# VectorE's pieces of linear attention two stick-breaking units further back in its program

## What is computed

```
z = einsum(q_blk, k) * scale;  mask = key_pos < q_pos
log_1m_beta = where(mask, log_sigmoid(-z), 0)
between = reverse_cumsum(log_1m_beta) - log_1m_beta
weights = where(mask, exp(log_sigmoid(z) + between), 0);  out = weights @ v

log_alpha = log_sigmoid(gd @ gate_up + gate_b) / 16
b = cumsum(log_alpha)                  # in each chunk of 64 frames
o_inter = (q * exp(b)) @ S
scores[t,s] = sum_k q[t]*k[s]*exp(b[t]-b[s])   for s <= t
S = S * exp(b_last) + (k * exp(b_last - b))^T @ v
o = head_rmsnorm(o_inter + scores @ v, norm_g) * silu(g)
```

## Time and profile before

| what | us |
|---|---|
| median of 3 runs | 1580.3 (1577.7 to 1583.3) |
| profiled execution, own time | 1584.14 |
| its span | 1582.4 |
| TensorE matmul busy, whole span | 1478.7 (93%) |
| VectorE busy, whole span | 661.9 (42%) |
| ScalarE busy, whole span | 523.8 (33%) |
| GpSimd busy, whole span | 305.2 (19%) |
| mean granted TensorE clock | 0.979 of full |

### The profile page before, as it was taken

How to read it: one execution, slowest core, us unless ns; L and a number is a source line. 1 busy time by engine, 2 the same in 40 slices (tenths; PEclk the granted TensorE clock), 3 DMA queues, 4 the chain that set the end, 5 groups by cost and what they waited for, 6 DMA issues and landing times.

```text
span 1582.4 us, 27309 instructions
## 1 busy us (share of the span) xinstructions
PE 1478.7 (93%) x11281; PEld 1143.1 (72%) x11281; DVE 661.9 (42%) x1058; ACT 523.8 (33%) x936; POOL 305.2 (19%) x412
## 2 busy tenths in 40 slices
PE   5989989989898898989999999999999999999997
PEld 4767767766676554554678788888888888888875
DVE  5244152646563253646275424232332424242336
ACT  4432231424223466777343303122120403021121
POOL 5574624413241251514000100000000000000000
PEclk9999989999999899999999999999999999999999
DMA  5554413423233603004332402112020202111015
GB/s 185 140 146 124 125 42 101 116 57 96 57 87 93 178 2 81 2 1 133 111 132 78 144 16 67 40 40 66 13 93 0 93 13 68 38 61 45 27 40 186
DMA packets 134793, 124.10 MB, mean 78 GB/s; under 512 B 20797, under 2 KB 112122, under 8 KB 134698
## 3 DMA queue, kind: packets, MB, share of 16 engines
q1 hardware_dynamic: 88192, 92.69, 19.0%
q10 hardware_dynamic: 46506, 30.04, 6.8%
HBM read 97.88 MB, written 24.84 MB: 78 GB/s over the span
## 4 chain that ended last, share of the span: by engine, by line
PE 46%; DVE 2%; ACT 1%; DMA 1%; issue 1%; POOLq 0%; SPq 0%; DVEq 0%; ACTq 0%
PE all_ps_b L1990 22%; PE all_ps_b L1967 21%; PE all_ps_b L1572 2%; DMA bk_acc<-in_w_out 1%; POOLq L1592 0%; DVE bk_acc L1855 0%; PE all_ps_b L1960 0%; ACT bk_acc L1758 0%; DVE bk_acc L1865 0%; DVE bk_w1L L1826 0%; DVE all_hL L1871 0%; DVE bk_acc L1851 0%; DVE bk_acc L1922 0%; DVE bk_acc L1925 0%; DVE all_gL L1897 0%
## 5 line engine op out<-in xcount | busy, mean ns | idle before, releaser
L1907 DVE TENSOR_TENSOR bk_acc<-bk_acc,all_ps_b 128x512 f32<-128x512 f32 x128 | 87.9, 687 | 285.3 <-PE all_ps_b L1990 285.3
L1967 PE MATMUL all_ps_b<-all_hH,bk_w1L 128*128 128x512 f32 x512 | 200.1, 391 | 5.1 <-PE all_ps_b L1990 2.2
L1990 PE MATMUL all_ps_b<-bk_w2H,all_gL 128*128 128x512 f32 x512 | 199.8, 390 | 2.5 <-DVE all_gL L1897 2.5
L1990 PE MATMUL all_ps_b<-bk_w2L,all_gH 128*128 128x512 f32 x512 | 199.9, 390 | 0.0
L1990 PE MATMUL all_ps_b<-bk_w2H,all_gH 128*128 128x512 f32 x512 | 199.8, 390 | 0.0
L1967 PE MATMUL all_ps_b<-all_hH,bk_w1H 128*128 128x512 f32 x512 | 199.3, 389 | 0.0
L1967 PE MATMUL all_ps_b<-all_hL,bk_w1H 128*128 128x512 f32 x512 | 199.2, 389 | 0.0
L1200 PE MATMUL fr_ps_F<-fr_hH,fr_wL 128*128 128x512 f32 (+1 forms) x416 | 174.8, 420 | 5.7 <-POOL fr_wL L448 5.5
L448 POOL TENSOR_TENSOR fr_wL<-fr_raw,fr_wH 128x256 fp32r<-128x256 f32 (+1 forms) x208 | 159.6, 798 | 32.6 <-ACT fr_wH L495 29.2
L1200 PE MATMUL fr_ps_F<-fr_hL,fr_wH 128*128 128x512 f32 (+1 forms) x416 | 164.4, 395 | 0.0
L1200 PE MATMUL fr_ps_F<-fr_hH,fr_wH 128*128 128x512 f32 (+1 forms) x416 | 164.3, 395 | 0.0
(11 more groups left out here) (339 smaller groups left out, 2234.9 us busy)
## 6 DMA issues: line engine op xcount, KB each, us to landing
fr_raw<-in_w_in ACTq DMA_DIRECT2D x37, 512.0 KB, 4.2
bk_raw<-in_w_ff SPq DMA_DIRECT2D x32, 512.0 KB, 4.3
all_raw<-in_w_ff SPq DMA_DIRECT2D x32, 512.0 KB, 4.8
projected<-fr_stage ACTq DMA_DIRECT2D x39, 256.0 KB, 4.4
fr_raw<-in_w_in SPq DMA_DIRECT2D x13, 512.0 KB, 4.2
fr_xt<-in_x SPq DMA_DIRECT2D x8, 512.0 KB, 5.3
bk_acc<-in_x SPq DMA_DIRECT2D x8, 512.0 KB, 3.3
x_after_mixers<-bk_acc SPq DMA_DIRECT2D x8, 512.0 KB, 2.7
```

The lines of the kernel that those rows point to most:

```text
L1907: dve.tensor_tensor(acc[:, j, ds], acc[:, j, ds], ybank[g % 4][:], ALU.add).then_inc(collected, 1)
L1967: m = pe.matmul(bank[s][h][:], w[s][:, k, :], a[:, k, hs], start=(k == 0 and q == 0), stop=(k == KB - 1 and q == 2))
L1990: m = pe.matmul(ybank[g % 4][:], a[:, i, ts], w[:, i, ds], start=(i == 0 and q == 0), stop=(i == FB - 1 and q == 2))
```

## The change

In VectorE's program of a unit, the linear attention pieces that are issued behind unit u are now those of slots up to u - 2 instead of u. The order of the pieces among themselves, their number, and the programs of all other engines stay. The largest slot is 28 + 26 = 54, so that the last pieces are now issued behind unit 56 of 72, which is unit 8 of the third pair.

```diff
@@ -2747,7 +2747,7 @@
                         scale(i - 1)
                     if i and u == LOW_AT:
                         mixed_low(i - 1)
-                    gla(i * NU + u)
+                    gla(i * NU + u - 2)
 
             for i in range(PAIRS):
                 if i:
```

## The result

| | before | after |
|---|---|---|
| median, us | 1584.16 (6 runs) | 1595.42 (6 runs) |
| lowest and highest, us | 1577.7, 1586.52 | 1591.55, 1599.8 |
| profiled execution: own time, span, us | 1584.14, 1582.4 | 1593.99, 1592.3 |
| mean granted TensorE clock | 0.979 | 0.979 |

The ratio is 1.0074, with a 95% interval of 1.0053 to 1.0096: slower by 11.7 us, 8.4 to 15.2. The direction is the one that was forecast. The time, 1595.4, lies above the forecast 1589.5 and 0.9 us above the upper end of the range. Two things add up to that: the three later runs of before were all at 1585 or more, which moved the base from 1580.3 to 1584.2, and the change cost 11.7 us where 9.2 were forecast. The second is not clear of noise, since 9.2 lies inside the interval of 8.4 to 15.2.

What follows compares the result with a forecast made beforehand. TensorE has almost no air in the stick-breaking and linear attention stage, so new waits cost time: 2.0 + 0.4 + 1.7 + 0.2 + 1.7 + 3.2 = +9.2 us on 1580.3 gives 1589.5 us, range 1582.5 to 1594.5.

Steps and rivals of the forecast that it cites:

- the other pieces: Rest of linear attention, both halves: TensorE finds operands ready within some tenths; +0.4 us (0 to 2).
- place 2: Second pair: earlier units gain, then a stall before transpose L2479 takes it back; +0.2 us, +1.7 for the clock.
- Place 1: First pair: transpose L2479 waits some 2.9 us for VectorE's k·exp product; +2.0 us, +1.7 for the clock.
- The gain ahead of the transpose: Second pair: with shorter waits on softplus, TensorE comes to transpose L2479 some 3.2 us earlier.
- what was gained is waited away: Second pair: the time gained is lost in one stall of some 3.2 us before transpose L2479.
- Place 3: Third pair, end of linear attention: gating 3.1 us later delays the projection's load and conversion L1560; +3.2 us (2.2 to 5).
- (a): Rival, chance 0.16: same waits, but the clock stays up behind them; +5.3 us, 1585.6.
- (b): Rival, chance 0.11: no price in the second pair, as ScalarE's exponentials run earlier too; +4.1 us, 1584.4.
- (c): Rival, chance 0.08: faster, VectorE waits go and ScalarE's conversion waits without holding TensorE; 1570.1 us.
- (d): Rival, chance 0.10: new waits larger by GpSimd's instruction (0.7), longer low clock at each stall; some +14 us, 1594.3.
- the forecast's 1.7: Clock loss behind a TensorE wait of 3 us before the transpose: +1.7 us each in first and second pair (0 to 3.4).

Runs made afterwards that it cites:

- the middle pieces alone: Only keys, state, takes and soft_g stand two units further back, against the kernel before: 1586.9 us, ratio 1.0019.
- the swap of the products: Full change plus VectorE's keys' product (L2355) put ahead of the queries' product (L2351), against the kernel before: 1594.5 us, ratio 1.0066.
- early pieces alone: Only soft, scan, to_last, diag0, diag1, qin, kout stand two units further back, against the kernel before: 1592.5 us, ratio 1.0044.
- the part kernels: Three kernels, each delaying only one group of VectorE's pieces by two units, against the kernel before: ratios 1.0044, 1.0019 and 1.0003.
- the end alone: Only both0, both1, result0, result1 stand two units further back, against the kernel before: 1586.6 us, ratio 1.0003.
- the kernel with only `SPLIT_AT` 9: Kernel before with ScalarE's conversion of the first loaded block one unit later (SPLIT_AT 8 to 9), against the kernel before: 1584.9 us, ratio 0.9991.
- the conversions later: Full change plus SPLIT_AT from 8 to 9, ScalarE's conversions one iteration later, against the kernel before: 1597.0 us, ratio 1.0077.
- the three slots put back: Full change with diag1, qin and kout one unit back instead of two, against the kernel before: 1594.4 us, ratio 1.0064.
- one unit: All pieces one unit further back instead of two, against the kernel before: 1580.9 us, ratio 0.9977.

## Why the prediction was right in direction and short in size

**What failed, in short.** The larger part of the miss is the base: with 1584.2 in place of 1580.3 the forecast of +9.2 us is 1593.4, and the range moved with it, 1586.4 to 1598.4, holds the 1595.4 measured. In the sum the term that was mis-sized is "the other pieces", +0.4 us, put in without stepping through them: 1.9 us by the landmarks, 3.0 (0.5 to 5.5) by the middle pieces alone. The three places were found and have the forecast's sign. In place 2 one step was wrong, and its net came out right by luck.

**Place 1, forecast +2.0 and +1.7: right.** TensorE waits 3.45 us before L2479 where 2.9 were forecast, and the stretch around it grew by 3.8 us against 3.7. VectorE's timeline there:

```profile
555.19 0.42 DVE L2739 SCALAR_TENSOR_TENSOR sb_SP<-sb_E,all_ps_b 128x256 f32<-128x256 f32 x1 [1.38 <-ACT sb_E L2653]
555.53 0.68 DVE L2346 TENSOR_TENSOR gla_A<-all_ps_b,gla_eye 128x512 f32<-128x512 f32 x1
556.13 0.84 DVE L2351 TENSOR_TENSOR gla_qin<-gla_qin,gla_q 128x512 f32<-128x512 f32 x1
556.89 1.09 DVE L2355 TENSOR_TENSOR gla_kout<-gla_kout,gla_k 128x512 f32<-128x512 f32 x1
```

Softplus 10 starts as logarithm 10 ends, then come the three operations, as stepped; they take 2.79 us instead of 2.48. The difference of 0.3 us goes with GpSimd, whose timeline is:

```profile
555.70 0.73 POOL L2589 TENSOR_TENSOR sb_R<-sb_R,sb_SP 128x256 f32<-128x256 f32 x1 [1.98 <-DVE sb_SP L2739]
556.75 0.70 POOL L2427 TENSOR_TENSOR gla_D<-gla_cum 128x256 f32<-128x256 f32 x1 [0.18 <-issue]
557.41 1.17 POOL L2428 TENSOR_TENSOR gla_D<-gla_cum 128x256 f32<-128x256 f32 x1
```

GpSimd's update is released by softplus 10, and its next instructions lie beside q·exp and k·exp, which took 0.84 and 1.09 us instead of 0.69. The Trainium skill, SBUF — State Buffer, "SBUF: two separate sides", has VectorE with two SBUF inputs and GpSimd reading SBUF lock one port pair and the loser wait for a whole instruction: the trace agrees in direction, but the loss was 0.15 and 0.4 us beside instructions of 0.70 and 1.17.

**Place 2, forecast +0.2 and +1.7: right in size, with one step wrong.** The stretch from L2516 to L2487 of the second half grew by 4.2 us, against 1.9, but part of that lies ahead of place 2. Four starts of the same instructions separate it:

| TensorE instruction | before | after | later by |
|---|---|---|---|
| L2516 | 598.11 | 602.45 | 4.3 |
| L2833, behind the first half's L2530 | 617.44 | 623.74 | 6.3 |
| L2817, sums 11 | 642.67 | 645.53 | 2.9 |
| L2820, sums 12, behind the transpose | 646.22 | 654.74 | 8.5 |

Between the first two lies the low clock around 613 to 625: 2.0 us, in no term of the forecast. The gain ahead of the transpose came out, 3.4 us (3.2 forecast). The stall and the clock behind it cost 5.7 us (5.1 forecast). Net it is +2.2 against +1.9.

The step that was wrong is that "what was gained is waited away". The early pieces alone gain only 1.7 us there (L2820 at 616.70 before and 619.32 with them, 2.6 later; sums 11 at 642.67 and 643.57, 0.9 later) and have the same wait of 4.19 us. So the stall does not depend on the gain, and that the two nearly cancel is chance. The forecast of 3.2 us for it was also 1.0 too low. The operations ahead of it are slower where they lie next to GpSimd's:

```profile
644.98 1.68 DVE L2728 TENSOR_TENSOR all_hL<-sb_outT,all_hH 128x1024 fp32r<-128x1024 f32 x1 [0.51 <-ACT all_hH L2636]
...
649.27 1.48 DVE L2355 TENSOR_TENSOR gla_kout<-gla_kout,gla_k 128x512 f32<-128x512 f32 x1
```

```profile
645.54 1.71 POOL L2589 TENSOR_TENSOR sb_R<-sb_R,sb_SP 128x256 f32<-128x256 f32 x1
...
648.79 1.41 POOL L2589 TENSOR_TENSOR sb_R<-sb_R,sb_SP 128x384 f32<-128x384 f32 x1 [0.26 <-issue]
```

The remainder took 1.68 us instead of 1.22, the keys' product 1.48 instead of 0.69: together 1.25 us, where the forecast put in a few tenths. That GpSimd is the cause is argued from the two timelines; the swap of the products supports it for the second.

The low clock around 613 to 625 was 0.54, 0.50 and 0.68 over three stretches of 4 us. That is 5.1 us of full-speed work over the whole time, or 4.2 us counted over TensorE's busy time alone, against 1.6 in the earlier trace rows. Whether the change causes that is open: of the part kernels, the early pieces alone show 1.00 in these stretches, the middle and the end alone about 5 us lost there, and the kernel with only `SPLIT_AT` 9 about 1.7.

**The other pieces, forecast +0.4 (0 to 2): mis-sized.** The landmarks show 1.4 + 0.5 = 1.9 us in the two halves, the four waits at L2504 in the trace 1.7, and the middle pieces alone cost 3.0 us (0.5 to 5.5). That the levels' operands are ready "within some tenths" was right for each, up to 0.90 us, but in a stage with no air each counts. This was estimated without stepping through them, and the forecast had no low clock behind so short a wait, which the middle pieces alone show once.

**Place 3, forecast +3.2: right in mechanism, near in size.** ScalarE's and SyncE's timelines answer to the earlier trace rows:

```profile
720.96 1.06 ACT L2284 ACTIVATE gla_osq<-gla_osq 128x1024 f32<-128x1024 f32 x1 [1.95 <-DVE gla_osq L2399]
731.51 1.04 ACT L1560 CAST all_hH<-all_raw 128x1024 fp32r<-128x1024 f32 x1 [7.04 <-DMA all_raw<-mixed]
```

```profile
728.02 12.31 SPq L1555 DMA_DIRECT2D all_raw<-mixed  x5
```

VectorE's pieces between them, which answer to the earlier trace rows:

```profile
719.04 1.28 DVE L2723 SCALAR_TENSOR_TENSOR sb_outT<-sb_O,all_col,sb_osq 128x1024 f32<-128x1024 f32 x1 [0.98 <-ACT sb_osq L2632]
720.24 0.68 DVE L2399 SCALAR_TENSOR_TENSOR gla_osq<-gla_lg,gla_osq 128x512 f32<-128x512 f32 x1
723.10 0.75 DVE L2405 SCALAR_TENSOR_TENSOR gla_O<-gla_O,all_col,gla_osq 128x512 f32<-128x512 f32 x1
```

The order is the forecast's: scaling, sum of logarithms, exponential (now waiting 1.95 us for it), gating, load, conversion. ScalarE's wait was forecast as 6 to 7 us and is 7.04, TensorE's as over 5 and is 5.51; the stretch grew by 2.6 us against 3.2.

**The rivals.** (a), the clock stays up, is out: 0.61 and 0.59 behind the two stalls. (b), the price of place 2 is absent, is out by its 4.19 us. (c), faster because ScalarE can wait without TensorE, is out by the 5.51 us. Of (d) one half came, stalls larger by 0.5 and 1.0 us next to GpSimd; the other, longer low stretches behind them, did not in the changed kernel: behind each 1.6 to 1.7 us were lost, as after 610 in the earlier trace rows.

**The sum.** By the landmarks of the two traces the 12.5 us from L2460 to the projection are 3.8 for place 1, 1.9 for the other pieces, 2.0 for the low clock around 613, 2.2 for place 2 and 2.6 for place 3; the forecast had 3.7, 0.4, 0, 1.9 and 3.2.

By the part kernels the change is 7.0 for the early pieces, 3.0 for the middle and 0.5 for the end, each interval about 2 to 2.5 us to either side. The forecast's terms do not sort cleanly into these, because the gain ahead of place 2 belongs to both: the 1.76 us wait goes with the end pieces, the 0.72 with the early ones. So only the middle term, 0.4, can be held against its kernel.

How much is low clock can be estimated from the span and mean granted clock of every run, span times (1 - clock). Over the 18 runs of the three kernels in which every piece is two units back (the change, the swap, the conversions later) it is 39.8 us, over 81 runs of the kernel before 34.6: +5.2 us, give or take 2.3, about half of the cost. The forecast had 1.7 + 1.7 + 0.5 = 3.9. The kernel with the three slots put back has 40.3 (6 runs), as much as those; in what is left of its span it is 2.8 us above the kernel before, where those are 4.6 to 6.2.

The base was off by 3.9 us (1580.3, then 1584.2), more than the sum (2.5 us).

## What to carry to other kernels

Where engines with fixed programs are chained in units, the slot of a piece is a lead with two ends: a later place unblocks the producer's own chain, and beyond the slack of its first consumer more of it turns into stalls at places where the trace of before shows none. Here one unit gave 3.6 us and two cost 11.7, so try the smallest step, and step every consumer once, also those late by tenths only: on TensorE, which has no air here, five waits of 0.16 to 0.90 us and the clock behind one of them went with +3.0 us (0.5 to 5.5). Take a base from more than three runs where the effect is of the size of their spread (1577.7 to 1583.3 here). The last piece of a chain that ends in a store and a load sets when the next stage's data arrive, and the engine that waits for them in program order hands its wait on: 7.0 us of ScalarE became 5.5 us of TensorE.

## What the hardware showed that was not expected

- VectorE's product of two 128x512 tiles took 0.68 us at its shortest, 0.84 and 1.09 beside GpSimd instructions of 0.70 and 1.17 us, and, beside one of 1.41, 1.48 in the changed kernel and 1.49 in the swap. GpSimd's addition of 128x256 took 0.73 us, but 1.71 beside VectorE's remainder of 128x1024, which took 1.68 then. In the kernel before the same two lay side by side as well, with 1.64 and 1.22 us. Shifting work in time changed its cost: VectorE's busy time of the whole program rose by 10.4 us with not one instruction more.
- Behind waits of 1.07, 1.22 and 1.82 us of TensorE before the transpose the granted clock stayed at 1.00; behind those of 2.44, 2.78, 2.96, 2.98, 3.45 and 4.19 it fell to 1.2 GHz, and 1.7 us of full-speed work were lost each time, which the forecast's 1.7 met. The length of the wait does not settle it: in the early pieces alone the first stall, 3.46 us, had twice that, 3.4 us, around it (0.50 over all of 558 to 562), and in the middle pieces alone 1.7 us were lost behind a wait of 0.90.
- At the end of the first pair (around 605 to 625 us) the low clock cost between 0 and 5 us in the profiled executions, with nearly the same work and waits there: 0 with the early pieces late, 1.7 before, 5.1 after.
